# Two-layer-norm trunk block: the MLP gate goes into the second weights, quarter sums go straight into the residual rows, late tokens load in two parts

## The reference

```python
mod = (silu(c) @ w_ada + b_ada)                  # shift, scale, gate of both sub-layers
u = layer_norm(x) * (1 + sc_m) + sh_m
z = u @ w_in                                     # pool, q, k, v, conv, three gates
merged = sum(sigmoid(z_gate[b] + b_gate[b]) * y[b] for b in range(3))
x = layer_norm(ALPHA * x + g_m * (merged @ w_o), ln_mix_g, ln_mix_b)
u = layer_norm(x) * (1 + sc_f) + sh_f
h = square(relu(u @ w_ff1 + b_ff1))              # 1024 -> 4096
x = layer_norm(ALPHA * x + g_f * (h @ w_ff2 + b_ff2), ln_ff_g, ln_ff_b)
```

## Time and profile before

| | |
|---|---|
| median of three runs | 1545.88 us |
| the profiled execution | 1547.44 us, span 1545.5 us |
| granted TensorE clock, mean | 0.979 of full |
| DVE, ACT, POOL busy | 62%, 38%, 27% of the span |
| DMA | 231 MB, 149 GB/s over the span |
| chain that ended last, by engine | PE 77%, DVE 14%, ACT 4%, issue 2%, DMA 2% |

### The profile page before, as it was taken

How to read it: one execution, slowest core, us unless ns; L and a number is a source line. 1 busy time by engine, 2 the same in 40 slices (tenths; PEclk the granted TensorE clock), 3 DMA queues, 4 the chain that set the end, 5 groups by cost and what they waited for, 6 DMA issues and landing times.

```text
span 1545.5 us, 17609 instructions
## 1 busy us (share of the span) xinstructions
PE 1457.3 (94%) x6802; PEld 1208.6 (78%) x6802; DVE 955.6 (62%) x1238; ACT 585.6 (38%) x814; POOL 410.8 (27%) x352
## 2 busy tenths in 40 slices
PE   7799899999997999999998998999999999999977
PEld 7687687878865888888877886888888888888855
DVE  3878688787955223222457778766666645446786
ACT  3312254554543111111243663444444544344141
POOL 1007400000002544542003425344443400004545
PEclk9999999999998999999999999999999999999988
DMA  9673011010003556554360274444445869456351
GB/s 349 225 263 120 28 30 36 14 36 28 15 14 121 180 189 206 184 186 157 97 230 28 82 242 167 150 150 151 155 151 179 277 247 330 176 201 218 109 204 55
DMA packets 154784, 230.97 MB, mean 149 GB/s; under 512 B 9240, under 2 KB 87246, under 8 KB 152664
## 3 DMA queue, kind: packets, MB, share of 16 engines
q1 hardware_dynamic: 142936, 179.67, 34.9%
q0 software_dynamic: 11776, 50.34, 8.9%
HBM read 171.22 MB, written 58.75 MB: 149 GB/s over the span
## 4 chain that ended last, share of the span: by engine, by line
PE 77%; DVE 14%; ACT 4%; issue 2%; DMA 2%; SPq 1%; ACTq 0%; DVEq 0%
PE ps L1791 22%; PE ps L1793 22%; PE ps L1792 22%; PE ps L1892 7%; DVE part_lo L1663 2%; PE ps L1811 2%; PE ps L1950 1%; DVE partial L1287 1%; DVE mid L1373 1%; DVE bn L1254 1%; DVE t_raw L1605 1%; PE ps L1992 1%; DMA u_scratch<-tmp 1%; DMA ada<-in_w_ada_dram 1%; DMA t_raw<-u_scratch 1%
## 5 line engine op out<-in xcount | busy, mean ns | idle before, releaser
L1791 PE MATMUL ps<-act_hi,w_hi 128*128 128x512 f32 (+1 forms) x512 | 198.9, 389 | 0.6 <-DVE act_lo L1323 0.6
L1663 DVE TENSOR_TENSOR part_lo<-k_raw,part_hi 128x1024 fp32r<-128x1024 f32 x112 | 157.3, 1443 | 63.8 <-ACT part_hi L835 61.6
L1793 PE MATMUL ps<-act_hi,w_lo 128*128 128x512 f32 (+1 forms) x512 | 196.4, 384 | 0.0
L1792 PE MATMUL ps<-act_lo,w_hi 128*128 128x512 f32 (+1 forms) x512 | 196.3, 383 | 0.0
L1791 PE MATMUL ps<-part_hi 128*128 128x512 f32 x448 | 177.2, 396 | 8.8 <-DVE part_lo L1663 8.8
L1792 PE MATMUL ps<-part_lo,part_hi 128*128 128x512 f32 x448 | 176.2, 393 | 0.0
L1793 PE MATMUL ps<-part_hi,part_lo 128*128 128x512 f32 x448 | 176.0, 393 | 0.0
L835 ACT ACTIVATE part_hi<-k_raw 128x1024 fp32r<-128x1024 f32 x112 | 116.7, 1059 | 122.4 <-DMA k_raw<-tw_scratch 61.2
L1458 DVE TENSOR_TENSOR w_lo<-w_raw,w_hi 128x1024 fp32r<-128x1024 f32 x30 | 44.2, 1474 | 175.4 <-ACT w_hi L835 175.4
L1791 PEld LDWEIGHTS ps<-act_hi,w_hi 128*128 128x128 f32 x512 | 96.5, 188 | 20.8 <-DVE act_lo L1323 1.4
L1793 PEld LDWEIGHTS ps<-act_hi,w_lo 128*128 128x128 f32 x512 | 96.5, 188 | 19.1
(11 more groups left out here) (237 smaller groups left out, 3296.9 us busy)
## 6 DMA issues: line engine op xcount, KB each, us to landing
k_raw<-h_scratch SPq DMA_DIRECT2D x112, 256.0 KB, 4.2
ada<-in_w_ada_dram SPq DMA_DIRECT2D x11, 2048.0 KB, 9.9
w_raw<-in_w_in_dram SPq DMA_DIRECT2D x42, 512.0 KB, 4.3
tw_raw<-in_w_ff_dram POOLq DMA_DIRECT2D x16, 1024.0 KB, 7.9
tw_scratch<-tw_sum POOLq DMA_DIRECT2D x16, 1024.0 KB, 4.7
h_scratch<-h_sum POOLq DMA_DIRECT2D x64, 256.0 KB, 2.5
k_raw<-tw_scratch SPq DMA_DIRECT2D x64, 256.0 KB, 5.4
pair_raw<-in_w_ff_dram SPq DMA_DIRECT2D x13, 1024.0 KB, 6.0
```

Of the source, the lines that this page charges most:

```text
L1663: nc.vector.tensor_tensor(part_lo[s][:, :, :], k_raw[rs][:, :, :], f(part_hi[s][:, :, :]), ALU.subtract)\
L1791: nc.tensor.matmul(out, sh, mh, start=first, stop=False)
L1792: nc.tensor.matmul(out, sh, ml, start=False, stop=False)
L1793: return nc.tensor.matmul(out, sl, mh, start=False, stop=last)
```

## The change

1. **Gate into the weights.** Per pair POOL now first multiplies all four blocks by the gate (two instructions of 128x1024, `gate_row`), makes the three sums and one difference in place, and stores seven blocks instead of four: 1 MB and 768 KB. `load_k` reads every right operand from there. For the first 13 pairs (`TWO_ROWS`) two load buffers alternate, and the next load is issued after the first multiplication, once the stores of the pair before have landed; the last three pairs use one buffer and load only after the stores of the pair before. The second buffer and the gate row lie where `mid` 5 to 7 will be written, so DVE waits for stores before `merge(5)` and `merge(6)` and for all sums before the last block. SP's wait ahead of the `w_o` rows becomes a wait for the last store. POOL also waits for `br_lo_done` at the start.
2. **Quarters into rows.** POOL adds `q1`, `q2`, `q4` to the residual rows early; `quads(3)` to `quads(5)` add PSUM straight to the rows. POOL's 16 gate multiplications at the end, `q12` and the late gate load go away. `end_tile` has one addition instead of multiplication and addition, and `finish_tile` of the tile before stands ahead of it.
3. **Late tokens in two parts.** Three of the late half's four tiles are loaded before the last tile is stored, the last one after.
4. **Norms spaced.** Tiles 0 to 3 are taken at q = 88, 91, 94, 97 with one step of q between statistics, root and norm. Their stores come after all part loads.

```diff
+TWO_ROWS = 13
+FIRST_NORM = 88
-            sp.wait_ge(tw_summed, 4 * FF_PAIRS)
+            sp.wait_ge(tw_stored, 32 * FF_PAIRS)
             for q in range(2):
                 load_row(q, w_o[0, q * P:(q + 1) * P, :])
...
+                if q == ST - 1:
+                    sp.wait_ge(u_stored[0], 16 * ST // 2)
+                    sp.wait_ge(u_stored[1], 16 * (ST // 2 - 1))
+                    load_u(t3_raw, 0, HALF, HALF - P)
+                    load_u(t2_raw, 1, HALF, HALF - P)
+                    sp.wait_ge(x2_end_done, 1)
...
-            for i in range(2):
-                sp.wait_ge(u_stored[i], 16 * ST // 2)
-            load_u(t3_raw, 0, slice(HALF, SEQ))
-            load_u(t2_raw, 1, slice(HALF, SEQ))
+            sp.wait_ge(u_stored[1], 16 * ST // 2)
+            load_u(t3_raw, 0, SEQ - P, P)
+            load_u(t2_raw, 1, SEQ - P, P)
...
                 load_k(q)
-                t = q - (PRODUCTS * FF_PAIRS - 6)
-                if 0 <= t < 4:
-                    sp.wait_ge(y_ready, t + 1)
-                    sp.dma_start(out_rows[t], y_tmp[t][:, :]).then_inc(stored[t], 16)
-            for t in range(ST // 2, ST - 1):
+            for t in range(ST - 1):
...
+            pool.wait_ge(br_lo_done, KT)
...
+            nc.gpsimd.dma_start(gate_row[:, :, :].rearrange("p h n -> p (h n)"), gate_dram[1:2, :].partition_broadcast(P))\
+                .then_inc(tw_in, 16)
+            load_rows(0)
             for p in range(FF_PAIRS):
+                rows, n = rows_of(p), 6 * p
+                pool.wait_ge(tw_in, 16 * (p + 2))
+                for i in range(2):
+                    pair = rows[:, 2 * i:2 * i + 2, :]
+                    nc.gpsimd.tensor_tensor(pair, pair, gate_row[:, :, :], ALU.mult).then_inc(tw_summed, 1)
+                    pool.wait_ge(tw_stored, 32 * p)
+                    if i == 0 and p + 1 < TWO_ROWS:
+                        load_rows(p + 1)
...
+                nc.gpsimd.dma_start(tw_dram[p, :, 0:4, :], rows[:, :, :]).then_inc(tw_stored, 16)
+                pool.wait_ge(tw_summed, n + 6)
+                nc.gpsimd.dma_start(tw_dram[p, :, 4:7, :], tw_sum[:, :, :]).then_inc(tw_stored, 16)
+                if TWO_ROWS <= p + 1 < FF_PAIRS:
+                    pool.wait_ge(tw_stored, 32 * (p + 1))
+                    load_rows(p + 1)
...
-            for quad, t0, half, ready in ((q12, 0, 1, 12), (q1, 0, 0, 16), (q4, 4, 1, 20), (q2, 4, 0, 24)):
+            for quad, t0, half in ((q1, 0, 0), (q2, 4, 0), (q4, 0, 1), (q4, 4, 1)):
...
-                    nc.gpsimd.tensor_tensor(quad[:, t, :], quad[:, t, :], gate_ff[:, cs], ALU.mult)\
-                        .then_inc(quad_added, 1)
                     nc.gpsimd.tensor_tensor(row, row, quad[:, t, :], ALU.add).then_inc(quad_added, 1)
...
+            for j in range(5, LAST):
+                for b in range(4):
+                    if b == 3:
+                        dve.wait_ge(tw_stored, 32 * (TWO_ROWS - (1 if j == 5 else 0)))
+                        merge(j)
+                    cut_gate_lo(j, b)
+            dve.wait_ge(tw_summed, 6 * FF_PAIRS)
...
-                nc.vector.tensor_tensor(tile[:, left], ps[:, quad_bank(6, t - 4), :], gate_ff[:, left], ALU.mult)\
+                nc.vector.tensor_tensor(row[:, left], ps[:, quad_bank(6, t - 4), :], row[:, left], ALU.add)\
                     .then_inc(end_acc, 1)
-                nc.vector.tensor_tensor(row[:, left], row[:, left], tile[:, left], ALU.add).then_inc(end_acc, 1)
...
-                n = q - 5 * FF_PAIRS - 2 * AHEAD
-                if 0 <= n < 4:
+                n, step = divmod(q - FIRST_NORM, 3)
+                if step == 0 and 1 <= n <= 4:
+                    finish_tile(n - 1)
+                if step == 0 and 0 <= n < 4:
                     take_tile(n)
+                elif step == 1 and 0 <= n < 4:
+                    scale_bias(N_ROOTS1 + n, n)
...
             for t in range(4, ST):
-                end_tile(t)
                 if t > 4:
                     finish_tile(t - 1)
+                end_tile(t)
```

More of the change, by code:

```diff
@@ L553, in load_k @@
                     sp.wait_ge(h_stored[p % 2], 48 * (p // 2 + 1))
[L554 to L557, removed]
+                n, w = ((0, 0), (4, 5), (3, 4), (6, 3), (1, 2), (5, 1), (2, 6))[i]
                 sp.dma_start(k_raw[q % RAWS][:, 0, :], h_dram[n, p]).then_inc(k_in[q % RAWS], 16)
-                sp.dma_start(k_raw[q % RAWS][:, 1, :], w).then_inc(k_in[q % RAWS], 16)
+                sp.dma_start(k_raw[q % RAWS][:, 1, :], tw_dram[p, :, w, :]).then_inc(k_in[q % RAWS], 16)
             def spill(t):
@@ L563, in spill, with load_u @@
                 sp.dma_start(resid_rows[t], mid[:, t, :]).then_inc(spilled if t < ST - 1 else spilled_end, 16)
-            def load_u(out, half, cs):
-                ks = slice(half * KT // 2, (half + 1) * KT // 2)
-                sp.dma_start(out[:, :, :], u2_dram[:, ks, cs]).then_inc(u_in, 16)
+            def load_u(out, half, first, n):
+                ks, to = slice(half * KT // 2, (half + 1) * KT // 2), slice(first % HALF, first % HALF + n)
+                sp.dma_start(out[:, :, to], u2_dram[:, ks, first:first + n]).then_inc(u_in, 16)
             for q in range(ST):
@@ L740, in _ @@
             pool.wait_ge(conv_done, 2)
-            for p in range(FF_PAIRS):
[L742 to L748, removed]
+            pool.wait_ge(br_lo_done, KT)
@@ L1228, in _ @@
                         copy(q1[:, t, :], ps[:, quad_bank(0, t), :]).then_inc(q1_saved, 1)
-                if 0 <= q - 5 * FF_PAIRS - 2 * AHEAD < 4:
-                    norm_tile(q - 5 * FF_PAIRS - 2 * AHEAD)
+                n, step = divmod(q - FIRST_NORM, 3)
+                if 0 <= n < 4 and step == 1:
+                    take_root(N_ROOTS1 + n, n)
+                elif 0 <= n < 4 and step == 2:
+                    norm(N_NORMS1 + n, n, y_tmp[n][:, :], resid)
             for t in range(ST // 2, ST - 1):
@@ L1482, in _ @@
             cut_gate_lo(0, 3)
-            with dve.Fori(1, LAST) as j:
+            with dve.Fori(1, 5) as j:
                 for b in range(4):
@@ L1705, in quads @@
                     dve.wait_ge(h_summed, 4 * FF_PAIRS)
+                elif i == 3:
+                    dve.wait_ge(quad_added, 12)
+                elif i == 5:
+                    dve.wait_ge(quad_added, 16)
                 dve.wait_ge(quad_done, n)
-                for out, other in ((), ((q2, q1),), ((q4, q2),), ((q12, q4),), ((q1, q1),), ((q4, q4), (q2, q2)))[i]:
-                    for t in range(4):
-                        nc.vector.tensor_tensor(out[:, t, :], ps[:, quad_bank(i, t), :], other[:, t, :], ALU.add)\
-                            .then_inc(quad_done, 1)
+                low, high = slice(0, HALF), slice(HALF, D)
+                for t in range(4):
+                    top_left, bottom_left = resid[:, t, low], resid[:, 4 + t, low]
+                    top_right, bottom_right = resid[:, t, high], resid[:, 4 + t, high]
+                    for out, other in ((), ((q2[:, t, :], q1[:, t, :]),), ((q4[:, t, :], q2[:, t, :]),),
+                                       ((top_right, top_right),), ((top_left, top_left),),
+                                       ((bottom_right, bottom_right), (bottom_left, bottom_left)))[i]:
+                        nc.vector.tensor_tensor(out, ps[:, quad_bank(i, t), :], other, ALU.add).then_inc(quad_done, 1)
             def take_tile(t):
-                dve.wait_ge(quad_added, 8 + 2 * (t + 1))
+                dve.wait_ge(quad_done, 12 + t + 1)
                 stats(resid[:, t, :], t)
-                if t >= 1:
-                    finish_tile(t - 1)
-                scale_bias(N_ROOTS1 + t, t)
             def finish_tile(t):
```

72 lines of the change are left out of this document (34 added, 38 removed).

## The result

The changed kernel takes 1555.23 us (median of ten runs, 1552.65 to 1557.51) against 1547.20 us for the kernel before (ten runs beside it, 1545.34 to 1551.38). The ratio is 1.0051, with a 95% interval of 1.0041 to 1.0061: **slower by 8 us**, where 6 us faster was forecast.

A forecast was written before the change was run, and what follows sets the result against it. PE was busy 94% of the span, so time could be won only where it waits or runs at the low clock. Terms -15.8 - 3.5 - 1.0 + 12 + 2 = -6.3 us from 1545.88 gave 1539.6, said 1539.8; range 1527 to 1556.

The forecast's parts named there:

- Mechanism of the gate stage: Gate stage: POOL's chain decides; SP's wait for its last store holds the w_o rows and last gate weights, so PE idles.
- T: Gate stage: time at which POOL's last store has landed, forecast 757 us, bounds 748 and 790.
- the clock behind the stand: Gate stage: PE restarts at the low clock level after its idle, some ten matmuls at twice 0.226, costing 2 us.
- the stand: Gate stage: PE idle before the last block's first gate product, waiting for weights, forecast 12 us.
- rival (b): Gate stage: POOL much later, kernel slower; stores of 7.2 us and loads of 6.8 give 1555; chance 0.24.
- S: Gate stage: landing of a pair's stores, forecast 6.4 us, bounds 5.9 and 8.2.
- The last product: Last product: PE's seven waits for DVE's low cuts vanish, winning 15.8 us, bounds 8 and 16.
- The forecast's sign: Last product: quads(5) would begin within 1 us of product 5's end.
- After the last matmul: DVE's chain after the last matmul shortens from 8.6 us, winning 3.5 us, bounds 1.5 and 3.7.
- Late tokens: PE's wait at 953 us: operands land near 927.8 against 928.9, winning 1.0 us, bounds -1.5 and 2.5.
- The sum: Whole kernel: -15.8 - 3.5 - 1.0 + 12 + 2 = -6.3 us against the profiled execution.

The follow-up runs named there:

- the kernel without the stand: Changed kernel with the w_o rows loaded straight into the free low branch buffer, not behind SP's wait for POOL's last store: 1526.25 us, ratio 0.9868.

## Why the prediction was wrong, point by point

**Mechanism of the gate stage: right.** The place (SP's queue ahead of the `w_o` rows), the sequence after T, the clock behind the stand and the 2 us it costs were all as written. The prediction's own sum with 25.2 in place of 12 gives 1554.3 for the profiled execution, which took 1553.65; that it comes so near is in part chance, as the first and third row of the balance (-3.8 and +1.6) are in none of its terms. The outcome is that of rival (b), a slower kernel, but not by the terms that it priced (S = 7.2, loads of 6.8): from first issue to landing a pair's stores took 6.31 us in the mean of the first twelve pairs. What held of (b) is its last reason, DVE's hold on POOL's operations.

**Size of T: wrong, and this is the step that failed.** The prediction said 15.2 us for each of twelve periods; it was 16.26. That is 12 x 1.06 = 12.7 us on T. The term S itself was right, 6.31 us from the first issue to the landing of both stores where 6.4 was said. Two other terms were too small:
- Between that landing and POOL's next issue lie another 0.47 us (6.78 from a pair's first store to the next load). The sum has no term for it.
- What follows, load issue, one multiplication and four sums, came out at 9.48 instead of 8.8: 0.68. Undisturbed it takes 8.54 (536.97 to 545.51 above), so contention with DVE cost 0.94 a pair, where 0.4 was allowed. The sums took 6.07 us a pair (groups of POOL's work after: 1.49, 1.53, 1.59 and 1.45 us in the mean), 1.28 each when clean. The 5.3 us read from the earlier trace rows for four sums should have been 5.15.

Counted from PE's restart at the gate stage, T came 14.3 us later than the forecast's sum (756.6 before rounding): 12.7 in the twelve periods, 1.1 before the first store, 0.7 in the last three pairs (23.3 against 23.1 each), and 0.2 less in the last landing. PE, counted the same way, was done with the branches 0.8 us later, so 12 became 25.2. What the execution of after was ahead before the gate stage (3.8 us) moved both alike and doesn't count.

The warning was in the trace. The earlier trace rows show a sum at 1.28 us, picked where POOL was alone; the mean over all 64 sums of before is 1.40 us, and periods of the same loop in before vary from 13.1 to 16.9 us with nothing else changed. A chain of sixteen passes has to be priced by the mean of its rows, not by a clean one. Even that mean falls short here, since the new multiplications brought contention of their own. T at 767 lies inside the bounds (748 to 790) and inside the likely span (749 to 775), but the chances put 0.64 on T up to 764 and only 0.24 on (b).

**What held POOL and DVE up.** The cuts, with two operands in SBUF, went from 1.53 us in the mean to 2.25 between 478 and 745 us, and POOL's sums from 1.40 to 1.52; the gate product, with one operand in PSUM, stayed at 1.22. The Trainium skill, SBUF — State Buffer, section Who interferes with whom, says just this: a VectorE instruction with two SBUF inputs contends with a GpSimd instruction that reads SBUF. By that rule, the trace agrees (2.25 us for the cuts, 1.22 for the gate product); the prediction had not used it, and its 0.4 us a pair were too few. The Trainium skill's rule that products belong on VectorE (GPSIMD Engine Reference, Engine selection), which was weighed, did not alter the forecast; no run here moved the products to DVE, so what that would give is not shown. The estimate from the Trainium skill for both stores together (DMA: Bandwidth & Descriptors), 6.2 us, is what 13 of the 16 pairs took from first issue to landing (6.2 to 6.3); the other three took 7.2 to 7.7.

**The last product: size right, causes wrong in part.** 15.8 us were forecast and no wait was left. But the norms' spacing, named first among the causes, is worth about 1 us by the traces and nothing that the times show (1554.7 us with bunched norms, 1555.2 spaced). The weight lies on POOL's multiplications (7 us) and, after that, on the stores among the loads (4 us). The forecast's sign, quads(5) within 1 us of product 5's end, failed: they began 3.5 us after it. The 20 cuts took 28.7 us instead of 24.6, and DVE stood four times for ACT, 1.12 us each; together that ate part of the 7 to 9 us of slack. It was still enough. (The shortest of the seven waits of before is 0.28 us; 0.96 is the first.)

**After the last matmul: right.** 4.8 us instead of 8.6, forecast 5.1.

**Late tokens: right in the mean, not in the profiled execution.** From tile 6's store to the first addition were 22.4 us instead of 23.3, 0.9 earlier as forecast (1.0). Over the fourteen traces the gain is 1.2 us (125.3 against 126.5 us for the stretch). In the profiled execution of the changed kernel nothing was left of it, as DVE's operations behind the landing took 25.7 us there and 24.5 in before; PE's wait stayed at 5.7. That these operations are long or short as they fall beside POOL's is the same term as above, left out of this step.

**The sum.** -15.8 - 3.5 - 1.0 is confirmed at -20.5 by the kernel without the stand. The +12 was +25.2. Taking the stand away gave 29.0 us where it and the low clock account for 27.2; PE's shorter wait for the late tokens there (4.3 instead of 5.7) is 1.4 of the rest.

## What to carry to other kernels

Where an engine off the critical path ends in a wait of a queue, list what stands behind that wait and ask whether it needs the awaited thing at all: here two loads needed the buffer, three stood there only by order, and giving the two a buffer that was free anyway was worth 29 us. Price a serial chain with the mean of many rows of the same form, contention in it, and look at the spread of its periods before trusting a clean row. When a sum of causes comes out right, each cause may still be wrong; only taking them out one at a time tells.

## What the runs showed of the hardware

- Operations of VectorE and GpSimd, both reading two tiles of SBUF, hold each other up: 16 of the 64 sums on POOL took 2.1 to 2.35 us instead of 1.28, a cut on DVE 2.25 in the mean instead of 1.23. In this row DVE's cut was issued just after a multiplication of 2.41 us had begun on POOL (546.65) and ended 1.09 us after it; the longest cut of the gate stage took 3.94 us:

```profile
546.70 3.45 DVE L1471 TENSOR_TENSOR w_lo<-w_raw,w_hi 128x1024 fp32r<-128x1024 f32 x1 [9.57 <-ACT w_hi L848]
```

- One MB and 768 KB issued one behind the other from POOL took 6.2 to 7.7 us from the first issue until both had landed; 768 KB with a sliver of the other took 4.1 to 5.1. With a pair every 11 us they took 6.6 to 10.6, though POOL did next to nothing else. POOL's next issue came 0.47 us after the landing.
- Runs of one kernel spread over up to 6 us here (before: 1545.0 to 1551.4 in all). In the profiled executions a part of it is the granted clock: behind PE's wait near 447 us it is 0.50 for 6 us in before and 1.00 in after, and PE restarts at the gate stage between 473.1 and 477.8 us, whatever the kernel. Parts worth 1 us can't be told from the times, but they can from a stretch that begins and ends at waits of PE and holds nothing else that changed.
